# One PSUM bank for the outputs of two attention units, three for the transposed probabilities, and the value products moved ahead of the transposes

## The reference, cut to what matters

```python
logits = jnp.einsum('nbqgrd,nbkgd->nbgrqk', qb, kb, preferred_element_type=jnp.float32) * ATT_SCALE + bias
probs, lse = _masked_softmax(logits, mask[None, :, None, None])
out = jnp.einsum('nbgrqk,nbkgd->nbqgrd', probs, vb.astype(jnp.float32))
```

## Time and profile before

| what | value |
|---|---|
| median of 3 runs | 2533.96 us (2529.08 to 2538.34) |
| the profiled execution | 2529.99 us, of which 2528.2 us is the span of its instructions |
| PE busy over the whole span | 2280.5 us (90%) |
| DVE, ACT, POOL busy | 968.5, 578.2, 464.9 us |
| mean granted clock of PE | 0.945 of full speed |
| the prompt attention stage | about 1074 to 1508 us of the span |

### The profile page before, as it was taken

The page is one execution under the profiler, slowest core; times in us unless marked ns, Lnnn a source line. Parts: engine busy times, 40 slices in busy tenths (PEclk is TensorE's granted clock), DMA queues, the critical chain, the costliest instruction groups (busy, mean ns, idle before and its releaser), DMA issues. The chain is left out here.

```text
span 2528.2 us, 34780 instructions
## 1 busy us (share of the span) xinstructions
PE 2280.5 (90%) x13808; PEld 1477.6 (58%) x13808; DVE 968.5 (38%) x2332; ACT 578.2 (23%) x1255; POOL 464.9 (18%) x664
## 2 busy tenths in 40 slices
PE   7999998999594689388888879999999999999998
PEld 3445666666362366255555554488888888844443
DVE  3001003333131354155555542267767675600110
ACT  3000002333121243155555541111111010100110
POOL 1313212221100355000121210013223322100000
PEclk9999998999787799799999899999999999999999
DMA  7712116775665789432123303156565642510110
GB/s 240 215 73 76 45 40 237 273 284 190 233 233 164 252 360 405 149 103 74 46 76 105 97 31 95 58 164 234 200 218 200 217 147 71 178 56 1 60 36 17
DMA packets 165878, 376.31 MB, mean 149 GB/s; under 512 B 47846, under 2 KB 104526, under 8 KB 147887
## 3 DMA queue, kind: packets, MB, share of 16 engines
q1 hardware_dynamic: 131964, 148.68, 18.8%
q0 software_dynamic: 25216, 149.43, 15.4%
q10 hardware_dynamic: 8538, 75.99, 8.7%
HBM read 345.71 MB, written 99.65 MB: 176 GB/s over the span
## 5 line engine op out<-in xcount | busy, mean ns | idle before, releaser
L2629 PE MATMUL ff_ps<-ff_hx,ff_aw 128*128 128x264 f32 x2464 | 552.8, 387 | 0.9 <-DVE ff_hx L2868 0.9
L2629 PEld LDWEIGHTS ff_ps<-ff_hx,ff_aw 128*128 128x128 f32 x2464 | 469.1, 191 | 81.6 <-issue 1.2
L337 PE MATMUL in_ps<-in_w,in_xT 128*128 128x512 f32 (+1 forms) x512 | 199.6, 545 | 0.0
L659 PE MATMUL pa_psT<-pa_ident,pa_L 128*128 128x128 f32 x816 | 129.4, 295 | 57.0 <-DVE pa_PT L817 46.9
L761 ACT ACTIVATE pa_L<-pa_L,pa_nm 128x128 f32<-128x128 f32 (+3 forms) x192 | 141.7, 740 | 84.9 <-DVE pa_nm L801 84.6
L791 DVE CUSTOM_DVE_ANT_0 pa_L<-pa_psS,pa_T 128x512 f32<-128x512 f32 (+3 forms) x288 | 138.3, 530 | 48.8 <-PE pa_psS L641 48.8
L659 PEld LDWEIGHTS pa_psT<-pa_ident,pa_L 128*128 128x128 f32 x816 | 92.0, 147 | 110.8 <-DVE pa_PT L817 52.6
L641 PE MATMUL pa_psS<-pa_kT,pa_qT 64*128 64x512 f32 (+3 forms) x576 | 122.8, 533 | 36.4 <-POOL pa_qT L708 35.6
L337 PEld LDWEIGHTS in_ps<-in_w,in_xT 128*128 128x128 f32 x512 | 95.2, 190 | 93.6 <-issue 84.9
L459 DVE TENSOR_SCALAR in_yout<-in_ps 128x512 f32<-128x512 f32 (+2 forms) x44 | 26.1, 593 | 300.3 <-PE in_ps L337 190.9
L1034 DVE COPY cmp_KT<-cmp_psT 128x512 f32<-128x512 f32 x128 | 88.5, 692 | 96.3 <-PE cmp_psT L950 96.3
(11 more groups left out here) (380 smaller groups left out, 3012.4 us busy)
## 6 DMA issues: line engine op xcount, KB each, us to landing
out_new_a_k_s<-in_cache_a_k ACTq DMA_DIRECT2D x8, 4088.0 KB
out_new_a_v_s<-in_cache_a_v ACTq DMA_DIRECT2D x8, 4088.0 KB
ff_aw<-in_w_up SPq DMA_DIRECT2D x44, 512.0 KB, 15.7
in_w<-in_w_in SPq DMA_DIRECT2D x5, 2048.0 KB
cd_X<-in_cache_a_k SPq DMA_DIRECT2D x8, 1024.0 KB
cd_X<-in_cache_a_v SPq DMA_DIRECT2D x8, 1024.0 KB
ff_hx<-in_w_down SPq DMA_DIRECT2D x14, 512.0 KB, 4.4
cd_X<-in_cache_a_k SPq DMA_DIRECT2D x24, 256.0 KB
```

The costliest lines, as they stand in the source:

```text
L337: mm = pe.matmul(ps[0:n, b, 0:width], xT[:, k, t * P:t * P + n], w[:, ch % WBUF, k, 0:width], start=(k == 0), stop=(k == KC - 1))
L659: mm = pe.transpose(psT[:, b % 2, (x - x0) * P:(x - x0) * P + P], L[:, u % 3, h, j * P:j * P + P], ident[:, :])
L2629: mm = pe.matmul(ps[:, bank_of(x, j, g), 0:H2], aw[:, j % 2, at, k, :], hx[:, bt, k, g * H2:g * H2 + H2], start=(k == 0), stop=(k == KH - 1))
```

## The change

`psO` becomes one bank that holds two halves of 256 columns, one for even and one for odd units, and `psT` gets the bank that this frees, so it has three. Three things follow in the code. Transposes of bank b wait for the copy of bank b - 3. values(u) waits for finish(u - 1) and no longer for finish(u - 2). In PE's loop values(s - 3) is put ahead of transposes(s - 2). The flipped gates are put at the start of the half of unit 8, so PE waits for their sigmoid before it writes the products of that unit, and ACT takes the sigmoid at the start of step 11, ahead of the copies. Nothing is added to or taken from the work.

```diff
@@ -554,8 +554,8 @@
         psS = m.ps("psS", [P, 2, 2, 512])
-        psT = m.ps("psT", [P, 2, 512])
-        psO = m.ps("psO", [P, 2, 512])
+        psT = m.ps("psT", [P, 3, 512])
+        psO = m.ps("psO", [P, 2, 2 * P])
@@ -647,16 +647,16 @@
                 for b in range(bank0[u], bank0[u + 1]):
-                    if b >= 2:
-                        na, nd = copied(b - 1)
-                        if on_dve(b - 2):
+                    if b >= 3:
+                        na, nd = copied(b - 2)
+                        if on_dve(b - 3):
                             pe.wait_ge(s_cd, nd)
                         else:
                             pe.wait_ge(s_ca, na)
...
-                        mm = pe.transpose(psT[:, b % 2, (x - x0) * P:(x - x0) * P + P],
+                        mm = pe.transpose(psT[:, b % 3, (x - x0) * P:(x - x0) * P + P],
                                           L[:, u % 3, h, j * P:j * P + P], ident[:, :])
@@ -667,13 +667,12 @@
-                if u >= 2:
-                    pe.wait_ge(s_wt, u - 1)
+                if u:
+                    pe.wait_ge(s_wt, u)
                 if u == QT:
                     pe.wait_ge(s_gl, 32)
-                    pe.matmul(psO[:, u % 2, 2 * P:2 * P + QT * 24], flip[:, :],
+                    pe.matmul(psO[:, u % 2, 0:QT * 24], flip[:, :],
                               gates[:, :, :].rearrange("p t n -> p (t n)"), start=True, stop=True).then_inc(s_gf, 1)
-                if u == QT + 2:
                     pe.wait_ge(s_gs, 1)
@@ -694,10 +693,10 @@
                     scores(s)
+                if s >= 3:
+                    values(s - 3)
                 if 2 <= s < U + 2:
                     transposes(s - 2)
-                if s >= 3:
-                    values(s - 3)
@@ -741,6 +740,10 @@
             for s in range(U + 3):
+                if s == QT + 3:
+                    act.wait_ge(s_gf, 1)
+                    nc.scalar.activation(gsig[:, :, :], psO[:, QT % 2, 0:QT * 24].rearrange("p (t n) -> p t n", t=QT),
+                                         ACT.Sigmoid).then_inc(s_gs, 1)
                 if 2 <= s < U + 2:
@@ -752,7 +755,7 @@
-                        nc.scalar.activation(PT[:, u % 3, x0:x0 + w], psT[:, b % 2, 0:w], ACT.Copy).then_inc(s_ca, 1)
+                        nc.scalar.activation(PT[:, u % 3, x0:x0 + w], psT[:, b % 3, 0:w], ACT.Copy).then_inc(s_ca, 1)
@@ -765,10 +768,6 @@
-                    if u == QT:
-                        act.wait_ge(s_gf, 1)
-                        nc.scalar.activation(gsig[:, :, :], psO[:, u % 2, 2 * P:2 * P + QT * 24].rearrange("p (t n) -> p t n", t=QT),
-                                             ACT.Sigmoid).then_inc(s_gs, 1)
                     nc.scalar.activation(Rs[:, u % 4, :], psO[:, u % 2, P:2 * P], ACT.Copy).then_inc(s_rs, 1)
@@ -814,7 +813,7 @@
-                    dve.tensor_copy(PT[:, u % 3, x0:x0 + w], psT[:, b % 2, 0:w]).then_inc(s_cd, 1)
+                    dve.tensor_copy(PT[:, u % 3, x0:x0 + w], psT[:, b % 3, 0:w]).then_inc(s_cd, 1)
```

## The result

The changed kernel takes 2603.43 us (median of 4 runs, 2599.98 to 2609.06), the one before 2533.91 us. The ratio is 1.0276, 95% interval 1.025 to 1.0301: slower by 70 us. The profiled execution took 2605.21 us.

The account below looks back on a forecast made before the run. No engine was full; a chain passing between PE, ACT and DVE set the steps. Loop +49, clock +16 and sigmoid +1 made +66 us: 2596 on the profile's 2530.0, 2600 us as median, range 2565 to 2650.

Parts of the forecast that it names:

- The mechanism: In the stage, values and transposes would lie between one finish and the next exponentials, where they had run beside logits and exponentials.
- The sum of the loop: Link lengths of the stage's new loop added per step: 41.7 us an iteration, 37.4 for the window; +49 us after corrections.
- clock term: PE's values and transposes at 1.2 GHz lengthen the loop by 1.4 us an iteration, +16 us for twelve.
- the two corrections: Adjustments to the loop: -1.2 us an iteration (-1.0 window) where DVE's last bank is not awaited; +0.75 for a fourth bank.
- the third rival: Clock falls, half of the stage at 1.2 GHz: 5 us an iteration instead of 1.4, 2644 us; chance 0.12.
- The second correction: A unit's fourth transposed bank waits for DVE's copy behind the logits: 1.3 us (n = 7), 1.0 (n = 6); +0.75 an iteration.
- The cover of the scores: PE's scores of the next unit, 1.77 us for seven blocks, are just hidden beside ACT's exponentials, 1.92 in the shortest case.
- The sigmoid: PE newly waits for the gates' sigmoid ahead of the values of unit 8: +1 us, between 0 and +2.
- The transposes' waits: PE's transposes waiting for DVE's copies of `psT` in the stage would fall from 46.9 us to under 15.
- The first rival: Faster: PE reaches values only after finish anyway, so the wait is free; gain 52 us, 2482 us; chance 0.05.
- The second: Gain and loss cancel: long steps win 1 us or more, short ones lose less; about 2534 us; chance 0.04.
- The rule on banks: PE writing and another engine reading one PSUM bank collide even at disjoint columns, so values must wait for the unit before.

Follow-up runs that it names:

- W: The kernel before with only the new wait: both outputs in one bank, two banks of transposes, transposes still ahead of values; ratio 1.0058.
- O: The kernel before with only values put ahead of transposes, two banks each and the old waits; ratio 0.999.
- R: The whole change, with the row `Rs` put ahead of the exponentials in ACT's loop; ratio to the kernel before 0.9713, repeated 0.9718.
- WT: The kernel before with the new wait and the third bank, transposes still ahead of values; ratio 0.9865.
- WTR: WT with the row `Rs` put ahead of the exponentials; ratio to the kernel before 0.9681, repeated 0.9676.
- F: R with `Rs` ahead of ACT's copies and finish right behind the logits on DVE; ratio to the kernel before 0.9642, 2443.50 us.

## Why the prediction was right, point by point

**The mechanism: right, shown.** The new loop was forecast as finish, values, transposes, last copy, exponentials, `Rs`, finish. The timeline shows it link by link, W and O show that neither wait nor order does it alone, and R shows that the loss is gone when the exponentials are taken out of it. Values waited 135.0 us for `finish`, in 79 of 95 steps, where some 100 us or more in nearly every step were forecast.

**The sum of the loop: right where the clock is full.** Forecast were 3.92 and 5.84 us for the steps with nk = 2 and 7; measured 3.88 and 5.85. Two small terms of the short step were off and cancel, which is luck: from the end of finish to PE's first product 0.15 us (1339.29 to 1339.44) for 0.06, and the row of `rgB` 0.17 us (1340.68 to 1340.85) for 0.26. For an iteration at full clock I had 41.2 us, for one of the window 36.4. The windows of the changed kernel, each from a finish to the eighth after, against the earlier trace rows:

```profile
1128.90:1175.70 46.80, 35.31 (x272) 24.75 (x272) 20.63 (x84) 20.06 (x53) 3.33 (x9) 0.85 0.12 38
...
1261.60:1307.30 45.70, 33.91 (x272) 24.00 (x272) 20.52 (x83) 20.06 (x54) 6.51 (x15) 0.89 0.15 38
1307.30:1348.70 41.40, 29.03 (x272) 20.42 (x272) 20.11 (x82) 20.82 (x55) 8.02 (x19) 1.00 0.22 63
...
1434.70:1472.90 38.20, 26.54 (x236) 18.61 (x236) 18.43 (x83) 17.87 (x52) 7.46 (x17) 0.96 0.48 161
...
1511.00:1551.40 40.40, 29.67 (x236) 21.13 (x236) 18.35 (x82) 17.98 (x52) 7.47 (x17) 0.87 0.09 26
```

The third of these rows, the sixth iteration, is at clock 1.00 and takes 41.4 us. The window kind takes 38.2 at 0.96, where loop and clock term made 37.8.

**The clock term: right in kind, too small.** It was put at 1.4 us for an iteration. The start of each finish to the start of the next gives 64 steps for the eight iterations with nk up to 8. In 45 of them the granted clock was 0.97 or more. They took 237.6 us, where the terms of the loop, without the two corrections, give 238.4. The other 19 had a lower clock and took 113.7 us, where the loop gives 93.4. So 20.3 us over the loop lie in steps that had time at 1.2 GHz: 2.5 us for an iteration, where 1.4 were forecast. It is a rough figure, since which banks DVE copies moves single steps by up to 1.3 us either way. A step with nk = 3 at either clock, and its values with nk = 8 at the lower one, against 1.97 us in the earlier trace rows:

```profile
1307.34:1312.52 5.18, 4.16 (x45) 2.98 (x45) 1.48 (x7) 1.95 (x6) 1.32 (x4) 1.00 0.81 263
1261.64:1268.44 6.80, 5.77 (x45) 4.43 (x45) 1.48 (x8) 1.95 (x6) 0.40 (x1) 0.75 0.34 100
```

```profile
1262.08 3.25 PE L680 MATMUL pa_psO<-pa_PT,pa_V 128*64 128x128 f32 x32 [2.46 <-DVE pa_tmp L828]
```

The step is longer by 1.6 us, just what PE's busy time grew by: nothing of it is hidden. The mean clock of the stage fell only from 0.94 to 0.92, well over the 0.85 that would have spoken against the forecast. So the third rival, half of the stage at 1.2 GHz, did not come, though what was held against it did not hold: PE's longest wait did not shrink from 3.5 us to 2.7, it was 3.9.

**The fourth bank: a term that was not there.** The second correction put 1.3 and 1.0 us on steps in which a unit has four banks and the first is DVE's, because the fourth then waits for DVE's copy. PE does wait there, 5 times and for 3.3 us in all. But the fourth bank of such a unit is DVE's as well, so the exponentials do not wait for it. A step with nk = 7 shows both:

```profile
1304.99 1.04 ACT L764 ACTIVATE pa_L<-pa_L,pa_nm 128x896 f32<-128x896 f32 x1
...
1305.43 0.66 PE L659 MATMUL pa_psT<-pa_ident,pa_L 128*128 128x128 f32 x4 [1.07 <-DVE pa_PT L816]
```

It takes 5.43 us, less than the 5.84 of the loop alone. This +0.75 us for an iteration was an error of reasoning. It hardly showed in the sum, because the steps in which the exponentials do wait for the last bank came out some 0.1 us longer than forecast.

**The total.** The stage grew by 82.1 us, where the sum had 66. The trace of before has the finish that ends the eighth iteration at 1379.8, the one of after at 1434.7. So the first eight took 290.4 us and take 351.3, +60.9 for a forecast of 51 with the clock and 1 for the sigmoid; the window's four grew by 21.2 for a forecast of 14. The term that is mis-sized is the clock's: the eight iterations take 43.9 us on the mean instead of 42.6, and four of them 43.4 to 46.8, outside the 40 to 43 that were forecast. The whole grew by 70 and not by 82, because a stage ahead ended 6 us earlier in this profile and runs differ by some us. That 2600 us lay so near to 2603 is therefore partly luck: what was forecast is 16 us too small, and the range held both.

**The cover of the scores: right in two iterations of three.** In the short step the scores (1341.16, 1.77 us) end just ahead of values at 1343.32. But where the only bank of the unit with nk = 1 is DVE's, the exponentials start early and so does finish: the step with nk = 2 then takes 2.74 us at full clock. The forecast took that as a gain of about 1 us. The scores then stick out, and the next step pays: in the first iteration they end 0.9 us after finish (1121.10 and 1120.18), at the lower clock 2.1 us after it (finish ends at 1383.76):

```profile
1382.90 3.02 PE L641 MATMUL pa_psS<-pa_kT,pa_qT 64*128 64x512 f32 x8
...
1385.85 0.44 PE L680 MATMUL pa_psO<-pa_PT,pa_V 128*64 128x128 f32 x4
```

This last step (nk = 7) takes 7.77 us for a forecast of 5.84.

**The sigmoid: about right.** The step that holds it takes 8.97 us, 3.1 over its forecast without it, of which some 0.9 is the scores that stick out. Before, the same step was 1.5 us longer than its like in the fourth iteration (8.21 for 6.71), and the next one up to 0.3. What is left is some 0.4 to 0.7 us, where +1 was put, between 0 and +2.

**The transposes' waits** fell under 15 us, as forecast (3.3). **Long steps** were to stay under 6.5 us: true for all with nk = 8 (5.76 to 6.08), but of the eight iterations' steps with nk = 7 three took more, 7.68 and 7.77 at a lower clock and 8.97 with the sigmoid. **Short steps** were to last 4 us and over: those with nk = 1 took 4.32 to 6.34, but four of eight with nk = 2 took less than 4, down to 2.74.

**The first rival, that it gets faster,** was to decide where PE comes to values after finish. PE waited in 79 of 95 steps. The second, that gain and loss cancel, wanted 0.5 us less in every step; at full clock the steps came out as summed. What the first missed, and I too, was what the third bank is worth if the order stays: WT is 1.3% faster.

**The rule on banks.** It was weighed as the reason why the wait cannot stay two units back. No run tried one bank with the old wait, so none here shows whether the rule holds. W shows the price of keeping it: 0.6% where transposes stand ahead of the wait.

## What to carry to other kernels

When two engines' slots are halved in one place to be doubled in another, follow the loop that closes through the halved slot, and ask what stands on each engine between release and re-use. A wait for the last user is cheap as long as independent work of the same engine stands ahead of it; moving that work behind the wait puts both on the loop. And the small instruction that releases a slot (here a row of 128 columns and a product) does not belong behind the long ones of its engine: with it early, both orders of PE gained, by 0.8% where the transposes still waited for their banks and by 1.8% or more where they did not or where values came first. Last, where PE's work lies on a loop, its lower clock is paid in full: here +1.6 us in a step of 5.2 us.

## What was not expected

The order of values and transposes alone is worth nothing within 0.3% (0.999, 0.9971 to 1.001), and the time from the first to the last finish is the same to 0.1 us, although the waits inside changed: 13 us less of DVE waiting for scores. And the effects of wait and order are far from a sum: 14.7 and 0.0 us alone, 103.5 together. Nor was the clock: it fell to 0.85 in one iteration of the change, and was 1.00 over the whole stage of R, WTR and F, and none of the expectations had counted on that.
